# Three chunk-tiles convolved on VectorE instead of two, evictions and the first short-convolution product on ScalarE: a two-layer streaming encoder on eight Trainium2 cores

## What is computed

```python
h = rmsnorm(x, norm_g)
proj = einsum("btd,de->bte", h, w_in)          # 13 x 1024 columns, split into the twelve below
(a_b, a_c, a_x, a_z, b_in, b_z, c_u, c_v, c_z, g_a, g_b, g_c) = split(proj)
# A: short convolution, 3 taps
y_a = a_b * causal_dwconv(prev_a, a_c * a_x, conv_a_w) * silu(a_z)
# B: long convolution, 31 taps per channel
glu = b_in[..., :W_B] * sigmoid(b_in[..., W_B:])
y_b = silu(layernorm(causal_dwconv(prev_b, glu, conv_b_w) + conv_b_b)) * silu(b_z)
# C: chunk MLP
y_c = gelu(c_u) * chunk_spatial_mix(layernorm(gelu(c_v)), w_s, b_s) * silu(c_z)
m = sigmoid(g_a) * (y_a @ w_br[0]) + sigmoid(g_b) * (y_b @ w_br[1]) + sigmoid(g_c) * (y_c @ w_br[2])
x = x + m @ w_out
```

## Time and profile before

| | us |
|---|---|
| three runs | 4301.25, 4305.78, 4576.11 (median 4305.78) |
| the profiled execution | 4298.67 |
| its span, slowest core (core 6) | 4297.1 |
| spans of the eight cores | 4275.0 to 4297.1 |

### The profile page before, as it was taken

How to read it: one execution, slowest core, us unless ns; L and a number is a source line. 1 busy time by engine, 2 the same in 40 slices (tenths; PEclk the granted TensorE clock), 3 DMA queues, 4 the chain that set the end, 5 groups by cost and what they waited for, 6 DMA issues and landing times.

```text
span 4297.1 us, 72177 instructions; the slowest of 8 cores (4275.0 to 4297.1 us)
## 1 busy us (share of the span) xinstructions
PE 4139.4 (96%) x24601; PEld 1941.1 (45%) x25036; DVE 2320.9 (54%) x3637; ACT 1578.3 (37%) x2586; POOL 211.9 (5%) x560
## 2 busy tenths in 40 slices
PE   7999999989989999999999999999999999999998
PEld 3444444444434444444444444444444444444443
DVE  3574444644367543774457743576437754377534
ACT  3254232262423622336252451325333362233622
POOL 0100000100000000100001000010001000010000
PEclk9999999999999999999999999999999999999999
DMA  9885678865777312452254422453235521345212
GB/s 164 155 175 139 159 202 187 177 140 139 179 212 181 123 69 88 154 150 95 77 176 136 138 75 79 144 148 112 79 113 183 137 107 69 124 135 161 76 69 94
DMA packets 186373, 571.56 MB, mean 133 GB/s; under 512 B 34224, under 2 KB 100256, under 8 KB 142496
## 3 DMA queue, kind: packets, MB, share of 16 engines
q1 hardware_dynamic: 151280, 377.40, 29.8%
q0 software_dynamic: 23712, 113.75, 13.5%
q10 hardware_dynamic: 11024, 75.76, 4.8%
HBM read 518.72 MB, written 128.05 MB: 151 GB/s over the span
## 4 chain that ended last, share of the span: by engine, by line
PE 85%; DVE 5%; issue 4%; DMA 3%; ACT 3%; SPq 0%; DVEq 0%; ACTq 0%; POOL 0%; POOLq 0%
PE ps L619 56%; PE ps L591 15%; PE ps L851 4%; PE ps L1260 4%; PE ps L1079 4%; ACT tmp_t L252 1%; DVE tmp_t L258 1%; ACT ya L252 1%; PE ps L683 1%; DVE tmp_t L255 1%; DVE co L255 1%; PE ps L1145 1%; DMA tmp_t<-x 1%; DVE co L735 1%; DVE tT L255 0%
## 5 line engine op out<-in xcount | busy, mean ns | idle before, releaser
L619 PE MATMUL ps<-hT,wring 128*128 128x512 bf16 x8837 | 2018.3, 380 | 46.1 <-DVE tmp_t L255 18.5
L619 PEld LDWEIGHTS ps<-hT,wring 128*128 128x128 bf16 x9088 | 877.7, 98 | 1088.6 <-issue 62.3
L255 DVE TENSOR_TENSOR tmp_t<-ps,tmp_t 128x512 f32<-128x512 f32 (+1 forms) x756 | 480.0, 637 | 991.5 <-PE ps L619 844.4
L252 ACT ACTIVATE tmp_t<-ps 128x512 f32<-128x512 f32 (+3 forms) x966 | 549.1, 584 | 893.6 <-PE ps L619 509.6
L591 PE MATMUL ps<-hT,wring 128*128 128x512 bf16 x3113 | 719.6, 382 | 21.0 <-ACT tmp_t L252 11.6
L252 ACT ACTIVATE tmp_t<-ps,pc 128x512 f32<-128x512 f32 (+1 forms) x432 | 277.0, 645 | 971.7 <-PE ps L619 916.5
L591 PEld LDWEIGHTS ps<-hT,wring 128*128 128x128 bf16 x3200 | 305.4, 98 | 359.7 <-issue 25.2
L252 ACT ACTIVATE tmp_t<-co 128x512 bf16<-128x512 f32 x256 | 157.4, 627 | 477.2 <-DVE co L262 464.8
L255 DVE TENSOR_TENSOR tmp_t<-tmp_t 128x512 f32<-128x512 f32 (+2 forms) x292 | 188.5, 645 | 184.7 <-ACT tmp_t L252 168.2
L735 DVE SCALAR_TENSOR_TENSOR co<-smp,co 128x512 f32<-128x512 bf16 x360 | 269.5, 748 | 24.1 <-DVE co L735 0.5
L252 ACT ACT_TABLE_LOAD x153 | 196.3, 1283 | 133.8 <-PE ps L591 31.5
(11 more groups left out here) (110 smaller groups left out, 2492.9 us busy)
## 6 DMA issues: line engine op xcount, KB each, us to landing
wring<-wbf SPq DMA_DIRECT2D x196, 1024.0 KB, 5.8
wring<-wblk POOLq DMA_DIRECT2D x76, 1024.0 KB, 13.2
wbf<-wring ACTq DMA_DIRECT2D x68, 1024.0 KB, 6.7
wring<-glp SPq DMA_DIRECT2D x258, 135.0 KB, 4.5
wring<-cwd SPq DMA_DIRECT2D x116, 256.0 KB, 5.4
tmp_t<-xp SPq DMA_DIRECT2D x56, 512.0 KB, 6.6
tmp_t<-x SPq DMA_DIRECT2D x32, 512.0 KB, 5.5
yp<-tmp_t POOLq DMA_DIRECT2D x24, 512.0 KB, 4.1
```

Source lines behind the costliest of these rows:

```text
L252: S.op("act", lambda e: e.activation(out=out, in_=in_, func=func, **kw), reads=reads, writes=writes)
L255: S.op(eng, lambda e: e.tensor_tensor(out=out, in0=in0, in1=in1, op=op), reads=reads, writes=writes)
L619: ins = e.matmul(outs[i], lhsT=wk(sl[i], kk, jj * 128), rhs=rr[i][:, kk, 0:NT], start=(kk == 0), stop=(kk == 7))
```

## The change

- `P.ew` gets a third chunk-tile, (1, 1), in passes 2 to 7. PE convolves 13 chunk-tiles of such a pass instead of 14, VectorE three. The ring loses that chunk-tile's slot and its five DMAs; `ew_start` issues one more DMA of POOL's queue.
- `smp` holds three data buffers instead of two. The weights move behind them, and there are two sets now (j = 0 and 1), so two `smp<-cwe` DMAs, on one lane: `Sched.op` lets a DMA wait for the one before it on its lane. They also wait for the sample's `co` and `v`, whose memory they now take.
- In passes 2 to 7 ScalarE evicts the convolution (`Identity` with the bias) instead of VectorE.
- In passes 2 to 7 ScalarE makes the first of the three products of the short convolution (`Copy` with a scale).
- `ew_pop(2)` now also stands behind each of the first 8 steps of a half, and behind each of the last 8 stands `ew_pop(4)` instead of `ew_pop(2)`.
- A method `Sched.finish` is added that nothing calls.

```diff
-                P.ew = ((0, 0), (1, 0)) if pr > 0 else ()
+                P.ew = ((0, 0), (1, 0), (1, 1)) if pr > 0 else ()
...
-                o = 600 + n * DEPTH * KB
-                DMA(smp[:, o:o + DEPTH * KB], cwe[j], (), ("xw",) + HR(SS) + RA(SS, "ya") + RA(SS, "yb"), "xw", eng="pool")
+                o = 820 + n * DEPTH * KB
+                DMA(smp[:, o:o + DEPTH * KB], cwe[j], (), ("xw",) + HR(SS) + RA(SS, "ya") + RA(SS, "yb") + sum((CO(SS, c) for c in range(NCH)), ()) + (R(SS, "v"),), "xw", eng="pool")
...
-            i = P.ew.index((T, j)) % 2
+            i = P.ew.index((T, j)) % 3
...
-                    TS(seg.co[:, j, 0:NT], bank_ap(b, NT), pcol(l, j, R_CBB), ALU.add, PSR(b) + ("pc",), CO(seg, j))
+                    if P.ew:
+                        ACT(seg.co[:, j, 0:NT], bank_ap(b, NT), AF.Identity, PSR(b) + ("pc",), CO(seg, j), bias=pcol(l, j, R_CBB))
+                    else:
+                        TS(seg.co[:, j, 0:NT], bank_ap(b, NT), pcol(l, j, R_CBB), ALU.add, PSR(b) + ("pc",), CO(seg, j))
...
-                            TS(ov, t[:, 2:2 + NT], pcol(l, j, R_CA + 2), ALU.mult, (rt, "pc"), (TR(seg, o),))
+                            if P.ew:
+                                ACT(ov, t[:, 2:2 + NT], AF.Copy, (rt, "pc"), (TR(seg, o),), scale=pcol(l, j, R_CA + 2))
+                            else:
+                                TS(ov, t[:, 2:2 + NT], pcol(l, j, R_CA + 2), ALU.mult, (rt, "pc"), (TR(seg, o),))
...
                         step()
+                        ew_pop(2)
...
                         step()
-                        ew_pop(2)
+                        ew_pop(4)
```

More of the change, by code:

```diff
@@ L125, in barrier, with finish @@
                 self.streams[e].append((waits, None, None))
+    def finish(self):
+        waits = [(e, self.count[e]) for e in self.ENG if self.count[e] > 0]
+        waits += [(("dma", lane), 16 * n) for lane, n in self.lane_n.items()]
+        kn = self.known["sp"]
+        self.streams["sp"].append(([(k, v) for k, v in waits if kn.get(k, 0) < v], None, None))
     def bank(self):
@@ L706, in ew_w @@
         def ew_w(l, j, k):
-            o = 600 + ew_j.index(j) * DEPTH * KB + l * KB + k
+            o = 820 + ew_j.index(j) * DEPTH * KB + l * KB + k
             return smp[:, o:o + 1]
```

## The result

The changed kernel is 1.0139 times as slow as before, with a 95% interval from 1.0103 to 1.0175: some 60 us, within the 2% that count as no change. Its profiled execution took 4360.23 us (span 4358.6, core 4) against 4298.67 before, +61.6 us where the forecast was +57.5.

A forecast was written before the change was run, and what follows sets the result against it. PE, busy 96%, was taken to bound the kernel, with VectorE's list stopping it at `finish`: -10.4 + 3.1 + 50.4 + 14.4 = +57.5 us on 4298.67, 4356 us (+1.3%); forecast 4330 to 4385, range 4308 to 4390.

The forecast's parts named there:

- -10.4 for PE's tile: Step 2 of half 1: PE loses one chunk-tile's convolution, saving 1.73 us in each of six passes.
- +50.4 for the stops: Stage A, `finish` matmul L916: PE waits 8.4 us a pass for VectorE's `split` subtraction, in six passes.
- +14.4 for the clock: Behind each PE wait at `finish` the granted clock falls, losing 2.4 us a pass.
- +3.1 for the second weight load: Start of pass 2: a second small load of tap weights delays the first tap, once, by 3.1 us.
- VectorE's list: From half 0's first multiplication to `split`'s subtraction VectorE needs 81.3 us; L916 could start after 72.9.
- that rival: `Identity` reloads ScalarE's tables for evictions ahead of `split`: 7.7 us a pass, 4402 us; chance 3%.
- that L916 is the one place, that it has 2 us to spare: Stage A: only at L916 does PE wait for a result behind VectorE's whole list, with 2 us to spare.
- PSUM adds nothing: Where VectorE frees a bank too late, PE only waits a little earlier for the same list: no extra time.
- The rule on additions and multiplications: Short convolution's first product: by the skill's rule it belongs on VectorE; keeping it there would lower the forecast 14 us.
- VectorE keeps up: Stage A: by busy time VectorE's added work fits, L916 doesn't wait, 4291 us; chance 10%.
- Half of it: No ScalarE delays at steps 3 and 7 and the clock holds: +29 us, 4328; chance 13%.
- second stop: VectorE's lag reaches a bank in half 1 or stage_bz's second `finish`: another 8 us wait, 4406 us; chance 5%.

The follow-up runs named there:

- spread kernel: Changed kernel, tile 1's two tap-wise chunks last and taps spread into half 1: ratio 1.0079; the 8.9 is from its variant with the first product on VectorE, 0.9988.
- run with two tiles: Changed kernel without the third chunk-tile on VectorE, product and evictions still on ScalarE: lowest run 4301.38 us (before, on the same chip, 4290.92).
- spread kernel with the product on VectorE: Changed kernel with taps spread into half 1, tile 1's tap-wise chunks last, first product back on VectorE: ratio 0.9988, lowest run 4285.28 us.

## Why the prediction came out right, and which steps did not

**The sum.** -10.4 for PE's tile: 8.9 in the spread kernel, where little else is in the way. +50.4 for the stops: the six stops sum to 39.6, and 18 smaller waits of over 0.3 us in half 0 and at the start of half 1 of passes 3 to 7 to 14.9, together 54.5. +14.4 for the clock: behind the six stops PE works 27.4 us at half clock, so it loses 13.7. These make 57.8 of the 60.7 us by which the rest has grown; 3 us I can't place. +3.1 for the second weight load: PE's wait at pass 2's gate went from 9.62 to 12.81, +3.2, and fell back in the run with two tiles. But it lies ahead of the gate, which the slowest core reached only 0.8 us later, so whether it lengthens the kernel isn't shown.

**VectorE's list** was the step on which most rested, and it held: 81.1 to 81.8 us measured, 81.3 laid out; steps of 4.64 to 4.71 against 4.68, 5.47 (once 5.82) and 6.25 at steps 3 and 7 against 5.5 and 6.2. Lines by form of the changed kernel (count, then busy time and mean ns):

```profile
L259 ACT ACT_TABLE_LOAD x153 | 196.3, 1283 | 112.6 <-PE ps L598 31.3 <-DVE tmp_t L262 25.5 <-PE ps L626 11.0
L265 DVE SCALAR_TENSOR_TENSOR tmp_t<-tT,pc,tmp_t 128x512 f32<-128x512 f32 x256 | 192.4, 751 | 106.6 <-ACT tmp_t L259 88.8 <-DVE tmp_t L265 0.9 <-DVE tmp_t L269 0.5
...
L259 ACT ACTIVATE tmp_t<-tT,pc 128x512 f32<-128x512 f32 x96 | 69.3, 722 | 300.9 <-DVE tT L262 300.9
...
L259 ACT ACTIVATE co<-ps,pc 128x512 f32<-128x512 f32 x78 | 52.7, 675 | 42.1 <-PE ps L858 42.1
```

The product takes 722 ns where 0.72 us was taken, the evictions 675 (before, the row nearest to them was 687). The table loads are 153 before and after, so `Identity` brings none; that rival falls. The Trainium skill (ScalarE: Activation LUTs, Table sets: the hidden batching unit) says so for the cheap functions, and the trace now agrees for `Identity`. In the second row are the 88.8 us that VectorE stood idle for the product, 0.93 each.

**What was wrong: that L916 is the one place, that it has 2 us to spare, and that PSUM adds nothing.** The trace of the kernel before already shows a second place. In each of the passes 2 to 7 the second projection of step 3 starts 0.26 us after the subtraction's end (2386.34 in pass 4), with 0.21 or 0.22 us of idle time that VectorE ends, and 1.72 us ahead of L916:

```profile
2386.60 1.89 PE L619 MATMUL ps<-hT,wring 128*128 128x512 bf16 x8 [0.21 <-DVE tmp_t L255]
```

Counted through the calls of `bank()`, this projection is handed the bank of the sums. So PE had no slack behind the subtraction, only a wait too short to be noticed. In the changed kernel chunk 1 of tile 1 takes no bank any more, the turn comes one bank later, and it is `finish` itself that gets the bank of the sums: there the operand and the bank wait for the same subtraction, and that trace can't tell them apart. The other runs can. With `finish` moved away the bank alone holds PE for 6.54 us, in the spread kernel for 4.1 to 4.6, and keeping that one bank out of the turn took 33 us from both kernels with VectorE's list unchanged.

That both roads lead to the same subtraction at the same matmul was luck for the forecast: the list's end fixed the stop either way. As forecast, PE also waited a little earlier for the same list: 39.6 us at `finish` and 14.9 ahead of it, against 50.4. But by the same working the spread kernel should have had 0 to 2 us of waiting a pass, and there the bank cost 4.1 to 4.6. That PE has "no slack" behind VectorE was true only of these orders of banks.

**The rule on additions and multiplications.** By the Trainium skill (ScalarE: Activation LUTs, Rules for kernel authors) the product should have stayed on VectorE, which the prediction priced at 14 us. The run with the product back agrees with the rule and more than doubles its worth: 33 us of the rest. The list lost 4.7 us a pass, not 2.4. Half of that is ScalarE's price, as forecast: a step takes 4.42 us instead of 4.65, about the difference between 722 ns and 487. The other half is the delays behind ScalarE's copies at steps 3 and 7, which went with the product. PE's stops fell by 9.5 us, its smaller waits by 14.6 and the loss by the clock by 2.5, 27 of the 33. The product took no work from VectorE, because the next instruction there needs it: VectorE stands idle for 0.92 us or more where the multiplication had taken it 0.49 and two gaps of 0.10 or 0.11.

**The other rivals.** "VectorE keeps up" names the right point of decision: the spread kernel with the product on VectorE shows that it does at a list of some 72 us. Its own count by busy time was what failed, since 0.93 us of idle for each product counts nowhere as busy. "Half of it" supposed shorter delays at steps 3 and 7; they came as laid out. No second stop showed in half 1 or at the second `finish` in stage_bz.

## To carry to other kernels

Before work is moved onto an engine with idle time, lay out its instruction list in order, hand-overs included, up to the one result that the bounding engine needs next, and ask for what else that result stands: an operand and a buffer that comes free with it are two roads to the same wait. When buffers are handed out in turn, a buffer given back by a late engine stops the early one, and keeping it out of the turn until its contents have been used may be worth as much as making the late engine faster (33 us each here). An operation in the middle of a dependent chain is the wrong one to give to another engine: the first engine stands idle for it all the same.

## What the runs showed of the hardware

- In the changed kernel VectorE stood idle 0.92 to 0.98 us for each product of 0.72 that it had given to ScalarE; a hand-over there or back took 0.09 to 0.15 us. From the end of VectorE's subtraction to the matmul that waited for it were 0.25 to 0.26 us.
- At the six places in stage A the granted clock stayed at 1.00 behind stops of 2 us and less and behind the one of 3.3 us, and was 0.50 for some us behind each of 4.1 us and more. The length alone doesn't decide: in pass 1 a wait of 2.81 us at one and the same matmul was followed by 0.50 in the traces of four kernels and by 1.00 in those of five, the one before and the changed one among them.
- At the start of pass 2, with transfers of 512 KB and 1 MB under way and a DMA share of 1.01 to 1.04, a store of 128 KB took 14.4 and 14.9 us, a load of 62 KB 11.9 and one of 31 KB 14.5. In the changed kernel, when these had landed, loads of 31 and of 135.5 KB took 2.2 and 2.3 us at a DMA share of 0.11 to 0.19.
